# Joined compress products, a norm shift in halves, and a reordered router in a two-block transformer kernel

## The chip, the core and the metric

The kernel runs on one core of one Trainium2 chip. The core has five engines with instruction streams of their own: TensorE (PE, matrix products and transposes; its weight loads are listed apart as PEld), VectorE (DVE), ScalarE (ACT), GpSimd (POOL) and SyncE (SP), which issues most DMAs. They wait for each other by semaphores. The metric is the device time of one execution in microseconds (us); lower is better.

## The reference

256 tokens of width 1024 pass through two layers of a first block and one layer of a second, all in fp32:

```python
for l in range(2):
    mix = retention(h, ...) if l == 0 else nsa_attention(h, ..., shared)
    h = layer_norm(ALPHA * h + mix, ln_mix_g[l], ln_mix_b[l])
    h = layer_norm(ALPHA * h + moe(h, ...), ln_ffn_g[l], ln_ffn_b[l])
# moe: 16 experts, each token's two are chosen inside the best of four groups
aff = sigmoid(x @ router_w);  sel_score = aff + router_b
y  += w[:, e:e+1] * ((silu(x @ w_gate[e]) * (x @ w_up[e])) @ w_down[e])
# nsa, ahead of layer 1's attention: 15 overlapping pieces of 32 tokens a group are compressed
blk = t[:, cidx] + pe;  k_cmp, v_cmp = gelu(blk @ w1) @ w2      # once for keys, once for values
```

The second block has an input projection of 8192 columns, two kinds of attention, a gated output, and a feed-forward part with a short convolution.

## The kernel before, in words

The 256 tokens are two tiles of 128 (`tt` 0 and 1). A weight matrix is read in blocks of 512 rows and 512 columns. Each block is split in two: ACT rounds it to a high part `whi` (L497), DVE subtracts that for a low part `wlo` (L503). The activations are split likewise into `th` and `tl`, so that a product of fp32 precision is the sum of three (whi x th, wlo x th, whi x tl), four of each for a block and a tile. `steady_tensor` runs such a stage; its first column group has line L698, the others L714. PE takes high parts from five places and raw or low parts from seven, in the order of the program.

Ahead of each stage the tokens are normalised and turned. `centre_half` takes mean and variance, ACT the square root (`root_half`, L817, after loading its table, L813), DVE the reciprocal (L821) and the shift (`shift_half`, L838), one instruction of 1024 columns for a tile. `half_turn_tensor` (L766) then transposes eight pieces of 128 columns; ACT copies them to `th` (L773, or L789 where a gain is applied), DVE subtracts to get `tl` (L781, L799). `opened_by` says at which steps of the next stage's first column group PE waits for them.

Behind the experts the order is: the last expert product (L1466), `centre_half` from the accumulators (L2825 to L2830), root, shift, turn of tile 0, the first column group's products for tile 0, turn of tile 1, the products for tile 1. The weights of the first two blocks are split by ACT there too, ahead of the table load.

At a router (`router_tensor_logits`, `router_vector`) PE forms 16 logits for a token from th and tl (L1127, L1132), turns tile 1 between the tiles, and then puts row sums of X into the accumulators (L1137). DVE takes the score (L1164), picks the experts in a chain of short operations up to `picked_r` (L1207), normalises their weights (L1212 to L1215), and builds selection matrices from slot numbers (L1218, L1236). PE gathers the tokens with them (L1403) out of `xn_h` and `xn_l`, the high and low part of X, whose low part DVE subtracts in two pieces (L2806). The experts' weights come through 20 places (`moe_homes`), each with a condition of its own; SP issues them in order.

The compress part (`nsa_in_tensor`, `nsa_beside_tensor`, L2113 and the lines around it) multiplies `cmp_x`, 60 columns of pieces, by four blocks of first-layer weights, in plain fp32, two for keys into one accumulator bank and two for values into another. The trace counts such a product as two instructions. Each half then has its own gelu on ACT (L2163), transposes (L2079) and second-layer product (L2091 for keys, L2098 for values). Between them stand transposes of queries (L2045), gate products (L2130) and the first attention scores (L2301). The order on every engine is written out by hand, by the counters `n` of the functions that stand beside a stage.

## Time and profile before

| what | before |
|---|---|
| median of 3 runs | 1333.68 us (1333.26 to 1333.89) |
| profiled execution: own time | 1332.24 us |
| profiled execution: span | 1330.1 us |
| PE busy | 1278.3 us (96%), 6630 instructions |
| PE weight loads | 890.9 us (67%) |
| DVE busy | 736.7 us (55%) |
| ACT busy | 541.0 us (41%) |
| DMA | 342.51 MB, 258 GB/s mean |

The span is the time between the first and the last instruction of the profiled execution; its own time has what lies around it. PE's busy time is modelled at the ends of products, so that a share of 96% still holds short waits. In the trace a row's first number is a start in us from the span's start, the second a duration; `x8` means eight instructions together, and the bracket the idle time of the engine ahead of the row and what ended it.

### The profile page before, as it was taken

How to read it: one execution, taken by the hardware profiler on the slowest of the kernel's cores; microseconds unless marked ns; L12 is line 12 of the kernel's file. 1: busy time of each engine (PE TensorE's matmuls, PEld its weight loads, DVE VectorE, ACT ScalarE, POOL GpSimd, SP SyncE). 2: the span in 40 equal slices, each digit the busy share in tenths (PEclk: the TensorE clock that was granted, in tenths of full speed). 3: DMA queues.
4: the chain of work that ended last, by engine and by line, in shares of the span. 5: the costliest groups of instructions: out<-in, count | busy, mean ns of one | idle time of the engine just before them, and what ended most of it. 6: DMA issues, size and time to landing. Idle time of an engine off the chain costs nothing.

```text
span 1330.1 us, 16620 instructions
## 1 busy us (share of the span) xinstructions
PE 1278.3 (96%) x6630; PEld 890.9 (67%) x6630; DVE 736.7 (55%) x1231; ACT 541.0 (41%) x791; POOL 74.9 (6%) x78
## 2 busy tenths in 40 slices
PE   9999998999999799998999999699999999999998
PEld 8887886444443477676444443378888887899986
DVE  4866657233222685876333322565674557688772
ACT  4455443111111443682111112455556655555551
POOL 0000000000000000000000000005770000000000
PEclk9999998999999899898999999899999999999999
DMA  9653588999999665407999999765455434655540
GB/s 335 234 177 127 159 343 328 407 420 421 421 422 417 217 202 188 183 17 301 393 421 421 421 421 421 283 190 165 148 159 160 157 127 149 215 167 183 190 158 32
DMA packets 103890, 342.51 MB, mean 258 GB/s; under 512 B 10188, under 2 KB 17020, under 8 KB 79100
## 3 DMA queue, kind: packets, MB, share of 16 engines
q1 hardware_dynamic: 100992, 336.30, 67.2%
q10 hardware_dynamic: 2812, 5.04, 1.1%
q8 instruction: 57, 0.93, 0.3%
q14 instruction: 29, 0.24, 0.0%
HBM read 340.27 MB, written 1.05 MB: 257 GB/s over the span
## 4 chain that ended last, share of the span: by engine, by line
PE 83%; DVE 10%; ACT 4%; issue 2%; ACTq 1%; DMA 0%; DVEq 0%; SPq 0%
PE PS L714 24%; PE PS L1421 17%; PE PS L1455 9%; PE PS L566 6%; PE PS L635 6%; PE PS L613 5%; PE PS L1403 2%; DVE wlo L503 2%; PE PS L1466 2%; ACT whi L497 1%; PE PS L698 1%; PE PS L2113 1%; PE PS L531 1%; PE PS L766 1%; PE PS L1866 1%
## 5 line engine op out<-in xcount | busy, mean ns | idle before, releaser
L503 DVE TENSOR_TENSOR wlo<-raw,whi 128x2048 fp32r<-128x2048 f32 (+1 forms) x122 | 272.9, 2254 | 106.2 <-ACT whi L497 101.8
L497 ACT ACTIVATE whi<-raw 128x2048 fp32r<-128x2048 f32 (+1 forms) x122 | 225.0, 1875 | 22.3 <-PE PS L613 13.9
L714 PE MATMUL PS<-whi,th 128*128 128x512 f32 x480 | 191.1, 398 | 1.2 <-ACT a_proj L3042 0.9
L714 PE MATMUL PS<-whi,tl 128*128 128x512 f32 x480 | 187.3, 390 | 0.0
L714 PE MATMUL PS<-wlo,th 128*128 128x512 f32 x480 | 186.9, 389 | 0.0
L1421 PE MATMUL PS<-moe_ring,xg 128*64 128x512 f32 x640 | 142.0, 593 | 2.6 <-DVE slot_sum L1579 2.6
L1421 PEld LDWEIGHTS PS<-moe_ring,xg 128*64 128x64 f32 x640 | 46.5, 137 | 91.6 <-issue 91.6
L1593 DVE TENSOR_TENSOR hidden<-hidden,PS 64x256 f32<-64x256 f32 x32 | 13.5, 423 | 170.0 <-ACT hidden L1536 170.0
L714 PEld LDWEIGHTS PS<-whi,th 128*128 128x128 f32 x480 | 90.2, 188 | 21.7 <-issue 2.0
L714 PEld LDWEIGHTS PS<-whi,tl 128*128 128x128 f32 x480 | 90.1, 188 | 19.2
L714 PEld LDWEIGHTS PS<-wlo,th 128*128 128x128 f32 x480 | 90.2, 188 | 17.5
L1563 DVE SCALAR_TENSOR_TENSOR y_split<-PS,w_slot,y_split 64x512 fp32r<-64x512 f32 x60 | 45.0, 749 | 93.7 <-ACT y_split L1519 92.8
L1536 ACT ACTIVATE hidden<-PS 64x512 f32<-64x512 f32 x32 | 18.9, 590 | 183.2 <-PE PS L1421 183.2
L566 PE MATMUL PS<-th,whi 128*128 128x256 f32 x288 | 81.7, 284 | 1.5 <-DVE wlo L503 1.5
L566 PE MATMUL PS<-th,wlo 128*128 128x256 f32 x288 | 81.5, 283 | 0.0
L566 PE MATMUL PS<-tl,whi 128*128 128x256 f32 x288 | 81.5, 283 | 0.0
L1519 ACT ACTIVATE y_split<-PS,w_slot 64x512 fp32r<-64x512 f32 x60 | 40.9, 682 | 97.1 <-PE PS L1455 96.4
L1455 PE MATMUL PS<-moe_ring,hT 128*64 128x512 f32 x320 | 72.6, 598 | 0.0
L903 POOL TENSOR_TENSOR rope_t<-b_proj,trig 128x256 f32<-128x256 f32 x48 | 41.5, 896 | 307.0 <-issue 294.0
L566 PEld LDWEIGHTS PS<-th,whi 128*128 128x128 f32 x288 | 55.3, 192 | 1.9 <-DVE wlo L503 1.4
L566 PEld LDWEIGHTS PS<-th,wlo 128*128 128x128 f32 x288 | 55.3, 192 | 0.0
L566 PEld LDWEIGHTS PS<-tl,whi 128*128 128x128 f32 x288 | 55.3, 192 | 0.0
(436 smaller groups left out, 2144.4 us busy)
## 6 DMA issues: line engine op xcount, KB each, us to landing
moe_ring<-in_moe_w_gate SPq DMA_DIRECT2D x40, 1024.0 KB, 13.8
moe_ring<-in_moe_w_up SPq DMA_DIRECT2D x40, 1024.0 KB, 15.9
moe_ring<-in_moe_w_down SPq DMA_DIRECT2D x40, 1024.0 KB, 19.3
raw<-in_w_in SPq DMA_DIRECT2D x32, 1024.0 KB, 5.3
raw<-in_ret_w_in SPq DMA_DIRECT2D x24, 1024.0 KB, 5.9
raw<-in_w_up SPq DMA_DIRECT2D x20, 1024.0 KB, 5.2
raw<-in_w_down SPq DMA_DIRECT2D x10, 1024.0 KB, 5.0
raw<-in_ret_w_out SPq DMA_DIRECT2D x8, 1024.0 KB, 5.1
```

The lines of the kernel that those rows point to most:

```text
L497: nc.scalar.activation(s.whi[:, high, 0:kc, 0:wide], s.raw[:, slot, 0:kc, 0:wide], ACT.Copy).then_inc(s.hi_done, 1)
L503: nc.vector.tensor_tensor(s.wlo[:, slot, 0:kc, 0:wide], s.raw[:, slot, 0:kc, 0:wide], s.whi[:, high, 0:kc, 0:wide], ALU.subtract).then_inc ...
L566: last = nc.tensor.matmul(PS[:, up_bank(j) + m // 2, (m % 2) * SEQ:(m % 2 + 1) * SEQ], w[:, k, c, m * P:(m + 1) * P], x[:, KC * kb + c, :] ...
L613: last = nc.tensor.matmul(PS[:, bank(j, tt), :], x[:, at, tt * P:(tt + 1) * P], w[:, k, c, :], start=(kb == 0 and c == 0 and i == 0), stop ...
L635: last = nc.tensor.matmul(PS[:, bank(j, tt), :], x[:, at, tt * P:(tt + 1) * P], w[:, k, c, :], start=(not opened and kb == 0 and c == 0 an ...
L714: last = nc.tensor.matmul(PS[:, 2 * (col % 2) + tt, 0:wide], x[:, KC * kb + c, tt * P:(tt + 1) * P], w[:, k, c, 0:wide], start=(kb == 0 an ...
L903: o(nc.gpsimd.tensor_tensor(t[i], u, v, ALU.mult))
L1403: last = nc.tensor.matmul(PS[:, bank, (c % 2) * SEQ:(c % 2 + 1) * SEQ], x[:, tt, c * P:(c + 1) * P], pick[:, g % 2, tt, :, :], start=(i == ...
L1421: m = nc.tensor.matmul(PS[64 * k:64 * k + 64, gate_up_bank(e), :], x, moe_place(layer, n)[:, c, :], start=(half == 0 and c == 0), stop=(ha ...
L1455: m = nc.tensor.matmul(PS[64 * half:64 * half + 64, down_bank_of(e), :], hT_of(e)[:, 2 * b + c, :], moe_place(layer, down_at(e) + b)[:, 2 ...
L1519: nc.scalar.activation(y_of(e)[rows, half, :], PS[rows, down_bank_of(e), :], ACT.Identity, scale=w_slot[rows, e:e + 1]).then_inc(s.y_hi, 1)
L1563: nc.vector.scalar_tensor_tensor(y_of(e)[low, half, :], PS[rows, down_bank_of(e), :], w_slot[rows, e:e + 1], y_of(e)[rows, half, :], ALU.m ...
```

## The change

Five things are edited.

1. The key and value products of the compress part go by turns into one bank, keys into rows 0 to 63 (60 and a pad of zeros), values into rows 64 to 123. One gelu, one pair of transposes and one group of copies serve both; both second-layer products stand behind the first half of the gate products. The four weight blocks are loaded as key, value, key, value.
2. The shift is two instructions of 512 columns with a semaphore each; the turn of the first half waits for the first. Behind the experts ACT loads the table ahead of the weight split, and takes the root between the two splits. In the first column group PE does the eight high-weight products of tile 0's second block, then the turn of tile 1, then the four low-weight products.
3. Behind each expert layer, 14 products of zeros stand ahead of the first turn.
4. At a router the row sums of tile 0 stand ahead of tile 1's turn; the low parts of X stand behind the picks, one ahead of each selection; the weights are normalised behind both selections. The `gains` place of the experts is used ahead of `rows`.
5. ACT issues the compress parameters behind the first weight split of the key stage, and two groups of parameters of the second block inside its input stage.

```diff
                      ("raw", 3), ("high", 1), ("raw", 4), ("high", 2), ("raw", 5), ("high", 3), ("raw", 6), ("high", 4),
-                     ("rows", 0), ("gains", 0), ("turned", 0), ("turned", 1)]
+                     ("gains", 0), ("rows", 0), ("turned", 0), ("turned", 1)]
...
+                    pe.wait_ge(half_lo, 4 * k + 1)
+                if step == 1:
                     pe.wait_ge(half_lo, 4 * k + 2)
-                if step == 1 and turn is not None:
+                if step == "turn":
                     turn()
...
+                        if tt == 0 and kb == 1 and high_first:
+                            pe.wait_ge(hi_done, b + 1)
+                            for c in range(KC):
+                                for x in (xh, xl):
+                                    nc.tensor.matmul(out, x[:, KC + c, 0:P], whi[:, b % HIGHS, c, :], start=False, stop=False)
+                            opening("turn")
+                            pe.wait_ge(lo_done, b + 1)
+                            for c in range(KC):
+                                last = nc.tensor.matmul(out, xh[:, KC + c, 0:P], wlo[:, b % RAWS, c, :], start=False,
+                                                        stop=(c == KC - 1))
+                            continue
...
+                    if half == 1 and late is not None:
+                        late(tt)
...
+        def normed_turn_tensor(pe, turn, k, tt):
+
+            half_turn_tensor(pe, turn, tokens(X), lambda tt: pe.wait_ge(half_normed, k + tt + 1), (tt,),
+                             lambda tt: pe.wait_ge(normed, k + tt + 1))
...
         def shift_half(tt):
-            nc.vector.scalar_tensor_tensor(X[:, tt, :], X[:, tt, :], small[:, 8 + tt:9 + tt], gb[:, 1, :],
-                                           ALU.mult, ALU.add).then_inc(normed, 1)
-
-        def layer_norm_halves(dve, st, o, k):
-
-            dve.wait_ge(params_in, 16 * st.params)
-            for tt in range(TT):
-                centre_half(o, tt)
-                inverse_half(dve, o, k, tt)
-                shift_half(tt)
+            for h, done in ((0, half_normed), (1, normed)):
+                x = X[:, tt, 512 * h:512 * h + 512]
+                nc.vector.scalar_tensor_tensor(x, x, small[:, 8 + tt:9 + tt], gb[:, 1, 512 * h:512 * h + 512],
+                                               ALU.mult, ALU.add).then_inc(done, 1)
...
+        def row_sums_tensor(tt):
+
+            for half in range(2):
+                last = nc.tensor.matmul(PS[:, 2 * tt + half, :], ident_a[:, :], X[:, tt, half * BW:(half + 1) * BW],
+                                        start=True, stop=False, skip_group_check=True)
+            return last
+
+        def busy(n):
+            zeros = nc.const_aps.tensor(0.0, [P, P], F32)
+            for _ in range(n):
+                nc.tensor.matmul(PS[:, 7, 0:P], zeros, zeros, start=True, stop=True)
...
                 if tt == 1:
-                    half_turn_tensor(pe, k, tokens(X), normed_by(pe, 4 * layer), (1,))
+                    pe.wait_ge(acc_free, 2 * (l_ret_out, l_nsa_out)[layer].n0 + 3)
+                    row_sums_tensor(0)
+                    normed_turn_tensor(pe, k, 4 * layer, 1)
...
-            for tt in range(TT):
-                for half in range(2):
-                    last = nc.tensor.matmul(PS[:, 2 * tt + half, :], ident_a[:, :], X[:, tt, half * BW:(half + 1) * BW],
-                                            start=True, stop=False, skip_group_check=True)
-            last.then_inc(rows_summed, 1)
+            row_sums_tensor(1).then_inc(rows_summed, 1)
...
+            def token_low(h):
+                dve.wait_ge(xn_h_done, 3 * layer + h + 2)
+                nc.vector.tensor_tensor(straight(xn_l, 1)[:, h], neighbours(X, 1)[:, h], straight(xn_h, 1)[:, h],
+                                        ALU.subtract).then_inc(xn_l_done, 1)
...
+            token_low(0)
+            inbox(dve, st)
+
+            o.then(nc.vector.scalar_tensor_tensor(rt2.rearrange("p t e -> p (t e)"), PS[:, 6, 0:TT * E], 1.0,
+                                                  picked_r[:, :, :].rearrange("p t e -> p (t e)"), ALU.add, ALU.mult))
+            selection(paired, 0, layer, rt2, 1)
+            token_low(1)
+            inbox(dve, st)
+            o(nc.vector.tensor_reduce(top[0][:, 0:1], PS[:, 7, 0:E], AX.X, ALU.max))
+            xg_copy(dve, paired, layer, 0, 1, first_bank(1))
+            selection(paired, 1, layer, rt2, 1)
             o.then(nc.vector.tensor_tensor(w_tok, affinity, picked_r[:, :, :], ALU.mult))
             o.then(nc.vector.tensor_reduce(top[2], w_tok, AX.X, ALU.add))
             o.then(nc.vector.reciprocal(top[3], top[2]))
-            o(nc.vector.tensor_tensor(w_tok, w_tok, wide(top[3], P, TT, E), ALU.mult))
-            inbox(dve, st)
-
-            o.then(nc.vector.scalar_tensor_tensor(rt2.rearrange("p t e -> p (t e)"), PS[:, 6, 0:TT * E], 1.0,
-                                                  picked_r[:, :, :].rearrange("p t e -> p (t e)"), ALU.add, ALU.mult))
-            selection(paired, 0, layer, rt2, 1)
-            inbox(dve, st)
-            o(nc.vector.tensor_reduce(top[0][:, 0:1], PS[:, 7, 0:E], AX.X, ALU.max))
-            selection(paired, 1, layer, rt2, 1)
             o(nc.vector.tensor_scalar(slot_no, rt2, -1.0, None, ALU.add))
+            o.then(nc.vector.tensor_tensor(w_tok, w_tok, wide(top[3], P, TT, E), ALU.mult))
             o.then(nc.vector.tensor_copy(w_split[:, :, :, 0], w_tok))
             o(nc.vector.tensor_tensor(w_split[:, :, :, 1], w_tok, w_split[:, :, :, 0], ALU.subtract))
             o(nc.vector.tensor_copy(slot_r[:, :, :], slot_no))
...
-                src = a["cmp_k_w1" if i < 2 else "cmp_v_w1"][D * (i % 2):D * (i % 2) + D, :]
+                src = a[("cmp_k_w1", "cmp_v_w1")[i % 2]][D * (i // 2):D * (i // 2) + D, :]
...
+                pe.wait_ge(tables_copied, COPIED_GELU)
+                for c in range(2):
+                    last = nc.tensor.transpose(PS[:, 7, 256 + c * P:256 + c * P + 124],
+                                               cmp_g[0:124, c * P:(c + 1) * P], cst[0:124, C_ID:C_ID + 124])
+                last.then_inc(tables_turned, 1)
...
-            for i in range(4):
-                k = i // 2
-                pe.wait_ge(lo_done, cmp_b0 + i + 1)
-                if i % 2 == 0:
-                    pe.wait_ge(cmp_built, BUILT_KW if k else BUILT_KS)
+            pe.wait_ge(cmp_built, BUILT_KW)
+            for h in range(2):
+                pe.wait_ge(lo_done, cmp_b0 + 2 * h + 2)
                 for c in range(8):
-                    last = nc.tensor.matmul(PS[0:60, 4 if k else 7, 0:CMP_HID], cmp_x[:, k, 8 * (i % 2) + c, 0:60],
-                                            cmp_block(i)[:, c, :], start=(i % 2 == 0 and c == 0),
-                                            stop=(i % 2 == 1 and c == 7))
-                last.then_inc(block_used, 1)
-                nsa_beside_tensor(pe, 10 + i)
+                    for k in range(2):
+                        last = nc.tensor.matmul(PS[64 * k:64 * k + 64 - 4 * k, 7, 0:CMP_HID],
+                                                cmp_x[:, k, 8 * h + c, 0:64 - 4 * k], cmp_block(2 * h + k)[:, c, :],
+                                                start=(h == 0 and c == 0), stop=(h == 1 and c == 7),
+                                                skip_group_check=True)
+                        if c == 7:
+                            last.then_inc(block_used, 1)
+            nsa_beside_tensor(pe, 12)
...
+            def keys_beside(n):
+                if n == 0:
+                    for dst, src in cmp_params():
+                        act.dma_start(dst, src).then_inc(tables_in, 16)
+                nsa_beside_scalar(act, n)
+            steady_side(act, l_nsa_kv, nsa_split_hi, nsa_kv_evacuate, keys_beside)
...
-            for b in range(AHEAD):
-                split_hi(act, sweep_first, moe_b0[layer] + b, 0)
             early_table(ACT.Sqrt)
+            split_hi(act, sweep_first, moe_b0[layer], 0)
+            root_half(act, 2 + 4 * layer, 0)
+            split_hi(act, sweep_first, moe_b0[layer] + 1, 0)
...
-            half_turn_tensor(pe, 2, tokens(X), normed_by(pe, 2), (0,))
-            nsa_in_tensor(pe, opened_by(pe, 2, lambda: half_turn_tensor(pe, 2, tokens(X), normed_by(pe, 2), (1,))))
+            busy(14)
+            normed_turn_tensor(pe, 2, 2, 0)
+            nsa_in_tensor(pe, opened_by(pe, 2, lambda: normed_turn_tensor(pe, 2, 2, 1)))
...
+            def a_in_beside(n):
+                if n == 1:
+                    params(act, st, a_params())
+                if n == 3:
+                    for dst, src in conv_params():
+                        act.dma_start(dst, src).then_inc(tables_in, 16)
+            steady_side(act, l_a_in, split_hi, take(l_a_in, lambda j, tt: a_proj[:, j, tt, :] if j < 2 else a_v[:, tt, :]),
+                        a_in_beside)```

On ACT, behind the experts of layer 0. `small` holds a token's statistics, `raw` the weight block as it came. Before:

```order
L497 ACTIVATE whi<-raw 128x2048 x2
L813 ACT_TABLE_LOAD
L813 ACTIVATE small<-cst 128x1
L817 ACTIVATE small<-small 128x1
L773 ACTIVATE th<-PS 128x4x128 x2
L817 ACTIVATE small<-small 128x1
L2734 DMA n_c<-in_c_nsa 128x292
L773 ACTIVATE th<-PS 128x4x128 x2
L3016 DMA cmp_pe<-in_cmp_pe_k 16x2x64 x2
L3016 DMA cmp_pe<-in_cmp_pe_v 16x2x64 x2
L3016 DMA cmp_w2k<-in_cmp_k_w 128x2x64 x2
L3016 DMA cmp_w2v<-in_cmp_v_w 128x2x64
```

After, from the same place on:

```order
L832 ACT_TABLE_LOAD
L832 ACTIVATE small<-cst 128x1
L499 ACTIVATE whi<-raw 128x2048
L836 ACTIVATE small<-small 128x1
L499 ACTIVATE whi<-raw 128x2048
L791 ACTIVATE th<-PS 128x4x128 x2
L836 ACTIVATE small<-small 128x1
L2771 DMA n_c<-in_c_nsa 128x292
L791 ACTIVATE th<-PS 128x4x128 x2
L499 ACTIVATE whi<-raw 128x2048
L2203 DMA cmp_pe<-in_cmp_pe_k 16x2x64 x2
L2203 DMA cmp_pe<-in_cmp_pe_v 16x2x64 x2
```

The table load went ahead of both splits, the root between them, and the compress DMAs behind the next split.

On PE, from the last query transposes' neighbours at the compress part to the first gate products. `cmp_g` is the gelu's output, `cst` holds the identity. Before:

```order
L2045 MATMUL PS<-cst,n_q 128x128 x8
L2113 MATMUL PS<-raw,cmp_x 60x256 x24
L2079 MATMUL PS<-cst,cmp_g 128x60 x2
L2045 MATMUL PS<-cst,n_q 128x128 x8
L2113 MATMUL PS<-raw,cmp_x 60x256 x8
L2091 MATMUL PS<-cmp_h,cmp_w2k 128x60 x2
L2130 MATMUL PS<-th,whi 48x256
```

After, from the last of 32 products by turns on:

```order
L2144 MATMUL PS<-raw,cmp_x 64x256
L2144 MATMUL PS<-raw,cmp_x 60x256
L2079 MATMUL PS<-cst,n_q 128x128 x8
L2117 MATMUL PS<-cst,cmp_g 128x124 x2
L2163 MATMUL PS<-th,whi 48x256
```

The products stand together; one pair of transposes serves keys and values; the second-layer product of the keys, L2091 before, is behind the first twelve gate products.

On DVE at a router, from the picks to the second selection matrix. Before:

```order
L1207 SCALAR_TENSOR_TENSOR picked_r<-route,tops 128x16 x2
L1212 TENSOR_TENSOR route<-route,picked_r 128x32
L1213 TENSOR_REDUCE tops<-route 128x2
L1214 RECIPROCAL tops<-tops 128x2
L1215 TENSOR_TENSOR route<-route,tops 128x32
L1218 SCALAR_TENSOR_TENSOR route<-PS,picked_r 128x32
L1236 TENSOR_TENSOR pick<-cst,route 128x256 x2
L1222 TENSOR_REDUCE tops<-PS 128x1
L1236 TENSOR_TENSOR pick<-cst,route 128x256 x2
```

After:

```order
L1236 SCALAR_TENSOR_TENSOR picked_r<-route,tops 128x16 x2
L1184 TENSOR_TENSOR xn_l<-X,xn_h 128x512
L1244 SCALAR_TENSOR_TENSOR route<-PS,picked_r 128x32
L1268 TENSOR_TENSOR pick<-cst,route 128x256 x2
L1184 TENSOR_TENSOR xn_l<-X,xn_h 128x512
L1249 TENSOR_REDUCE tops<-PS 128x1
L1589 COPY xg<-PS 128x512
L1268 TENSOR_TENSOR pick<-cst,route 128x256 x2
L1252 TENSOR_TENSOR route<-route,picked_r 128x32
```

One low part of X stands ahead of each selection, and the normalising of weights behind both.

## Rows read from the trace of the kernel before

**Rows 1.** PE's waits: what waited for what, us in total, times, longest.

```profile
PE PS L766 <- DVE X L838: 16.0, 4, 5.1
...
PE PS L698 <- DVE tl L799: 2.6, 1, 2.6
```

**Rows 2.** Timeline behind the experts of layer 0: start us, us, engine, line, operation.

```profile
440.97 3.71 ACT L497 ACTIVATE whi<-raw 128x2048 fp32r<-128x2048 f32 x2
...
444.33 1.27 DVE L2830 SCALAR_TENSOR_TENSOR X<-PS,small,gb 128x1024 f32<-128x1024 f32 x1
...
446.52 1.28 DVE L838 SCALAR_TENSOR_TENSOR X<-X,small,gb 128x1024 f32<-128x1024 f32 x1
...
448.17 1.97 PE L766 MATMUL PS<-cst,X 128*128 128x128 f32 x8 [5.05 <-DVE X L838]
...
450.80 0.69 DVE L781 TENSOR_TENSOR tl<-PS,th 128x512 fp32r<-128x512 f32 x1 [0.16 <-ACT th L773]
...
455.63 2.28 DVE L503 TENSOR_TENSOR wlo<-raw,whi 128x2048 fp32r<-128x2048 f32 x1
...
462.24 3.72 ACT L497 ACTIVATE whi<-raw 128x2048 fp32r<-128x2048 f32 x2 [4.34 <-issue]
```

**Rows 3.** The chain of waits in order of time: start us, us, what.

```profile
227.88 4.10 PE PS L1403 x32
...
255.65 6.87 PE PS L1421 x32
...
451.60 4.74 PE PS L698 x12
...
466.69 5.73 PE PS L714 x24
...
530.15 1.41 PE PS L2130 x12
...
874.04 27.48 PE PS L714 x120
```

**Rows 4.** Timeline of DVE behind the experts of layer 1.

```profile
856.10 2.16 DVE L799 SCALAR_TENSOR_TENSOR tl<-PS,small,th 128x128 fp32r<-128x128 f32 x8 [0.50 <-ACT th L789]
...
861.19 1.28 DVE L838 SCALAR_TENSOR_TENSOR X<-X,small,gb 128x1024 f32<-128x1024 f32 x1
```

**Rows 5.** Timeline of PE and DVE at the compress part.

```profile
514.12 10.57 PE L2113 MATMUL PS<-raw,cmp_x 128*60 128x256 f32 x48
...
518.60 0.42 DVE L892 TENSOR_TENSOR n_q<-rope_t 128x256 f32<-128x256 f32 x1
...
524.88 1.09 PE L2045 MATMUL PS<-cst,n_q 128*128 128x128 f32 x8
...
529.50 0.66 PE L2091 MATMUL PS<-cmp_h,cmp_w2k 128*128 128x60 f32 x4
...
533.19 1.29 DVE L2455 TENSOR_REDUCE n_top<-PS 128x2 f32<-128x512 f32 x2 [0.47 <-PE PS L2310]
...
534.61 1.10 PE L2098 MATMUL PS<-cmp_w2v,cmp_hr 128*60 128x64 f32 x16
...
536.16 1.13 PE L2301 MATMUL PS<-n_kp,n_qT 64*128 64x512 f32 x4 [0.45 <-ACT n_gT L2006]
```

**Rows 6.** Timeline: a weight load of an expert, value products of attention.

```profile
255.48 0.14 PEld L1421 LDWEIGHTS PS<-moe_ring,xg 128*64 128x64 f32 x2 [0.28 <-issue]
...
551.13 1.09 PE L2349 MATMUL PS<-n_pT,n_vp 128*64 128x128 f32 x16
```

**Rows 7.** Timeline of DVE and PE at the router of layer 0.

```profile
218.61 2.08 DVE L2806 TENSOR_TENSOR xn_l<-X,xn_h 128x512 fp32r<-128x512 f32 x2 [0.32 <-ACT xn_h L2785]
...
220.43 5.07 PE L1137 MATMUL PS<-X,small 128*128 128x512 f32 x8
...
220.62 0.23 DVE L1164 TENSOR_REDUCE route<-PS 128x32 f32<-128x64 f32 x1
```

**Rows 8.** One window: PE, PEld, DVE, ACT, POOL busy, PE's granted clock, DMA.

```profile
222.00:224.00 2.00, 2.00 (x4) 0.78 (x3) 1.77 (x11) 0.00 (x0) 0.00 (x0) 0.69 0.70 287
```

117 lines of the change are left out of this document (48 added, 69 removed).

## The prediction

> **What bounds the kernel now.** I read the page first: TensorE (PE) is busy for 96% of the span, so a change can win only where PE stands still or where it does less. The view of PE's waits says where it stands still, and no DMA is named there. Four turns of a normalised tile wait for the shift L838 (16.0 us in all), and the first products behind the experts of layer 1 wait 2.6 us for a low half [rows 1]. In the rows behind layer 0 [rows 2] the reader is to see one chain: ScalarE (ACT) splits two weight blocks (440.97, 3.71), only then loads the table for the square root, VectorE (DVE) has had the centred tile since 445.60 (444.33 + 1.27) and starts the shift at 446.52; the turn follows at 448.17. DVE then does a low split (2.28 each), two low halves of the turned tile (the second ends at 451.49), and 4.14 later, at 455.63, the next low split. The chain of waits [rows 3] shows PE's side: 12 products from 451.60 in 4.74, and the next column group at 466.69. The same shape stands behind layer 1 [rows 4]. Last I read the compress products [rows 5] beside other products of half width [rows 6], and the router [rows 7, 8].
>
> **The change part by part.** All times below are of the profiled execution (own time 1332.24, span 1330.1); the median of the runs is 1333.68, 1.44 above it.
>
> *Behind the experts, layer 0.* The table load and the root go ahead of the second weight split, so the root is ready before DVE has centred the tile. The shift then starts 0.20 behind 445.60 (a reciprocal between), at 445.8, and not at 446.52. It comes in two halves of about 0.65 (half of 1.28 [rows 2]), so the turn of the first half starts near 446.8, and copying to the high half is done before DVE has its low split behind it: 447.1 + 2.28 = 449.4. The low halves take 0.69 each: 449.4 to 450.8. PE's opening now waits for the first one alone, so it starts at 450.1 instead of 451.60. The second low split follows as before 4.14 behind the low halves, at 454.9, and ends at 457.2. Before, PE did 36 products behind that split: 12 of tile 0, 24 of tile 1. Now the eight products of high weights of tile 0 and the turn of tile 1 stand ahead of the wait for the split; the two low halves of tile 1 go on to 458.6, and 24 products at 0.229 (27.48 for 120 [rows 3]) end at 464.2. The next group stood at 466.69. Gain 2.4. It is set by DVE, so that it hardly depends on the clock: with the opening products at the 0.395 that the 12 of [rows 3] show (the granted clock was down for part of them), the loss is about 1.0. What is late next is the low split of the block after the next. Seven DMA issues on ACT, for which it did nothing else for 4.34 ahead of the split at 462.24 [rows 2], are moved between the two splits of that row (1.86 each). The first split now stands at 457.9, behind the copies of tile 1's turn; the issues, some 4.9 with the one that lay beside the copies, run to 464.7, the second split to 466.6 and its low half to 468.9. PE wants that at 464.2 + 24 x 0.229 = 469.7. I price it at nothing; if the cover of 0.8 is gone, it costs as much as the issues run over.
>
> *Fourteen zero products ahead of the first turn.* The trace counts an fp32 product as two instructions, so 28. Bounds: half of the 0.22 of a 256-column instruction (10.57 for 48 [rows 5]) is 0.11, 3.1 in all; a transposing instruction of that width takes 0.136 (1.09 for eight), 3.8. PE is free from 443.1 (448.17 less the wait of 5.05 [rows 2]), so they end between 446.2 and 446.9, and the turn is ready at 446.5 to 446.8. I take nothing; the far end costs 0.4, and at half clock 3.
>
> *Behind the experts, layer 1.* The same steps. The shift moves 0.7 up; the eight low halves (856.10 to 858.26 [rows 4]) follow the low split, whose place moves as far, and now run 855.0 to 857.2. PE starts after four of them, near 856.2. The second shift, 2.93 behind the low halves in the old rows (861.19 less 858.26), stands at 860.1, its low split ends at 863.65, the low halves of tile 1 at 865.85, and 24 products at 0.229 end at 871.4. The next group stood at 874.04 [rows 3]. It also needs its own high and low parts; the DMA issues that stood ahead of them on ACT are moved behind, so those end near 870.5. Gain 2.5; 0.6 less if all products run at half clock.
>
> *Joined compress products.* Before: 64 instructions with 60 output columns, 0.22 each, 48 of them together [rows 5], the other 16 after two groups of transposes. Now keys go to rows 0 to 63 of one bank and values to rows 64 to 123, by turns. No row of before shows this shape. The nearest on one side is the experts' first product, which goes to two halves of a bank by turns: 6.87 for 32 instructions of 512 columns, 0.215 each [rows 3], half of the 0.44 that twice the 0.22 would be, and its weight loads come in twos [rows 6]. On the other side the value products of attention, of 128 columns and by turns to two halves too: 16 in 1.09, 0.07 each against 0.11 [rows 6]. Between 128 and 512 columns lies 256: 0.108 each, 3.5 for a half of 32. The other bound is the old 0.22. I take 0.108, since both neighbours run at that pace. From 514.12: first half to 517.6. The second half waits for marks that DVE gives only behind the rope of the second query group, which ends at 519.0 (518.60 + 0.42 [rows 5]); so it runs 519.2 to 522.7. Then the query transposes 1.09, the gelu's two (0.3), twelve gate products 1.41, both second-layer products 0.66 and 1.10, and the first scores 1.13 [rows 3, 5]: 528.4, and with hand-overs the maximum L2455 at 529.0. It stood at 533.19 [rows 5]. Gain 4.2. The second-layer product of the values (1.10) is only moved up, ahead of the first scores, and it is in the sum on both sides: I put nothing more for its absence later, where PE stands between softmax steps.
>
> *Routers, both layers.* Three edits help the score L1164, at 220.62 [rows 7]: the shift in halves (0.65), the low halves of X (2.08 from 218.61, to 220.69) out of DVE's way, and row sums on PE ahead of tile 1. They bring 1.2 to 1.9 in each layer. Two things go back. One low half (1.04) now stands behind the picks; what left that place (four short operations that normalise weights, each below the 0.23 of L1164, together some 0.7) doesn't cover it, so 0.3 is lost. And the eight row sums (5.07 from 220.43) ran until the picks were nearly done; the granted clock was 0.69 in 222 to 224, on its way back [rows 8], and the gather that follows took 4.10 for 32 [rows 3], 0.128 each. Now four of them are gone from there, PE stands idle for some 3 us before the gather, and I expect part of the gather at half clock, which loses about 1.3, a third of its 4.10. Sum per router 0.1, both 0.2; bounds -1 and +2 each. The expert blocks' transfers aren't among PE's waits, and the order of two of their places is changed so that one starts earlier: nothing.
>
> Sum: 2.4 + 2.5 + 4.2 + 0.2 = 9.3. 1332.24 - 9.3 = 1322.9; against the median 1333.68 - 9.3 = **1324.4**.
>
> The Trainium skill ("TensorE: Matmul & The Clock Gate", Part 3: Packing small matmuls, The mechanism) says that a weight load overlaps products in flight only where the row groups differ. Both halves of the joined product use the same 128 rows. By that rule loads and products would stand one after another. The rows of the experts' product, also on the same rows, speak against it: 0.215 a piece, with the loads inside it; the trace does not agree with the rule here.
>
> **The rivals.**
>
> *A: the clock comes back for the gather.* The row sums ahead of tile 1 fill PE's wait for the shift; if the clock doesn't fall there, the logits take less and the gather keeps its 4.10. For it: PE's rows before the fall are dense. Against it: three short idle stretches remain. It gives 1.3 back in each layer and some 0.5 of the logits: 3.7 more, 1320.7.
>
> *B: the joined products run one after another.* For it: no row has 64 and 60 columns by turns at 256. Against it: the experts' pairs [rows 3]. 64 x 0.22 = 14.1 from 514.12 end at 528.3 rather than 522.7: 5.6 less, 1330.0.
>
> *C: slower than before, by loads that are not hidden.* Place: the 64 joined instructions. Each then costs its load (0.14 for two of the experts' [rows 6], taken here for one) and its columns (0.22): 64 x 0.36 = 23.0, ending at 537.1, 14.4 less: 1338.8. The kernel is slower than before once the products end 9.3 later than forecast, at 532.0: a pace above (532.0 - 514.12) / 64 = 0.28. Against it: with loads of as many columns the experts' pairs take 0.215 for twice the moving columns.
>
> **How the numbers follow.** The forecast as reckoned 0.62, with a range of its own of 1321 to 1328 (the half-clock prices of both layers' ends, 1.6, on one side, and the routers' bounds); A 0.12, B 0.12, C 0.04; 0.10 for several terms short at once, 1328 to 1334. A measurement of this kernel tells changes above 0.2% (2.7 us) from none: faster is under 1331.0. Faster: 0.62 + 0.12 + 0.09 of B + 0.04 of the rest = 0.87. Same: 0.03 of B and 0.05 of the rest, 0.08. Slower: C and 0.01, 0.05. Range 1319.5 to 1330: A below and the near half of B above are in it, C is not.
>
> **What would show it.** In the profile of the changed kernel: the four waits for the shift (16.0 in all) shrink to under 5, those behind the experts to near zero, as PE has zero products there; the next column groups stand 2.4 and, from the same stage's start, 2.5 nearer to the last expert product; 64 compress instructions span about 8.6 with a gap of 1.6 in the middle; the gather takes over 5 where A is wrong and 4.1 where it is right. The prediction is wrong if the compress products take over 12, if PE waits for a weight block behind the moved DMA issues, or if the zero products end after the shift's first half.

## The result, and the profile of the changed kernel

| | before | changed |
|---|---|---|
| median of 20 runs, us | 1333.62 (1331.81 to 1335.18) | 1335.85 (1334.61 to 1340.75) |
| profiled execution: own time, span | 1332.24, 1330.1 | 1336.96, 1335.2 |
| ratio, 95% interval | | 1.0018 [1.0012, 1.0025] |

The change made the kernel 0.18% slower. The forecast was 1324.4, so 11.5 us are missing (14.1 between the profiled executions, 1336.96 against 1322.9).

In the kernel before, the last expert products of the two layers stood here, so that the turns came 5.06 behind their ends, 443.11 and 848.71:

```profile
441.94 1.17 PE L1466 MATMUL PS<-y_last,pickT 128*128 128x512 f32 x4 [1.31 <-DVE y_last L1563]
...
847.54 1.17 PE L1466 MATMUL PS<-y_last,pickT 128*128 128x512 f32 x4 [1.31 <-DVE y_last L1563]
```

Behind the experts of layer 0 the timeline of the changed kernel (start us, us, engine, line, operation) reads as follows; it answers to [rows 2]:

```profile
443.33 1.16 PE L1499 MATMUL PS<-y_last,pickT 128*128 128x512 f32 x4 [1.31 <-DVE y_last L1598]
...
448.17 1.28 DVE L2863 SCALAR_TENSOR_TENSOR X<-PS,small,gb 128x1024 f32<-128x1024 f32 x1 [2.37 <-issue]
...
449.67 5.42 PE L1140 MATMUL PS<-const-float32-0.0 128*128 128x128 f32 x28 [5.18 <-issue]
...
454.93 1.04 PE L784 MATMUL PS<-cst,X 128*128 128x128 f32 x8
...
470.86 0.39 PE L730 MATMUL PS<-whi,th 128*128 128x512 f32 x1
```

PE's last expert product ends at 444.49. Then it waits 5.18, and the wait bears no engine's name but "issue": time in which the engine waited for nothing that the profile shows. Only then do the zero products run, for 5.42, and the first turn stands 10.44 behind the experts, where it stood 5.06 behind them. DVE has a wait of the same kind, 2.37. The last row is the first product of the next column group, at 466.69 before [rows 3]. Layer 1 answers to [rows 4]:

```profile
845.64 1.16 PE L1499 MATMUL PS<-y_last,pickT 128*128 128x512 f32 x4 [1.32 <-DVE y_last L1598]
...
851.93 2.71 PE L1140 MATMUL PS<-const-float32-0.0 128*128 128x128 f32 x11 [5.13 <-issue]
...
856.25 4.00 PE L1140 MATMUL PS<-const-float32-0.0 128*128 128x128 f32 x17 [1.60 <-issue]
...
860.04 1.09 PE L784 MATMUL PS<-cst,X 128*128 128x128 f32 x8
...
880.57 0.39 PE L730 MATMUL PS<-whi,th 128*128 128x512 f32 x1
```

Here the wait comes twice, once ahead of the zero products and once in their midst, and the turn stands 13.24 behind the experts. PE's waits answer to [rows 1]; of the 16.0 us for the shift 1.2 are left, as forecast, and 11.9 without a named engine stand in their place:

```profile
PE PS L1140 <- issue: 11.9, 3, 5.2
...
PE PS L784 <- DVE X L859: 1.2, 2, 0.6
```

The chain of waits (start, us, what) answers to [rows 3]: the gathers of the two layers, and the 24 products that end the first column group in either layer (of a new line, L714; the next column group is L730):

```profile
227.09 6.26 PE PS L1436 x32
...
465.29 5.73 PE PS L714 x24
...
629.13 6.60 PE PS L1436 x32
...
873.38 7.35 PE PS L714 x24
```

The compress part answers to [rows 5]. From the first joined product to the maximum L2492 it takes 532.94 - 518.22 = 14.72, against 533.19 - 514.12 = 19.07:

```profile
518.22 3.67 PE L2144 MATMUL PS<-raw,cmp_x 128*64 128x256 f32 x32
...
523.79 3.67 PE L2144 MATMUL PS<-raw,cmp_x 128*64 128x256 f32 x32 [1.90 <-DVEq L2065]
...
532.94 1.29 DVE L2492 TENSOR_REDUCE n_top<-PS 128x2 f32<-128x512 f32 x2 [1.57 <-PE PS L2346]
```

Taken by stages between the two profiled executions (plus is lost): up to the last expert product of layer 0 +1.4, from there to the next column group +2.8, compress and attention -6.4 (4.35 of it the compress part), router and experts of layer 1 +0.3, the end of layer 1's experts +8.4, the rest -1.4. The sum, +5.1, is the difference of the spans.

### The profile page after: what moved, and what is told of

Its sections match the earlier page's. It is cut to its first block, busy times and chain, and to the rows that moved or that the text cites. A ratio compares the mean times of both kernels' runs of the same rounds, so it can differ in the third digit from the quotient of the medians.

```text
span 1335.2 us, 16742 instructions
## 1 busy us (share of the span) xinstructions
PE 1280.2 (96%) x6684; PEld 895.0 (67%) x6684; DVE 738.0 (55%) x1240; ACT 540.9 (41%) x790; POOL 74.9 (6%) x78
## 4 chain that ended last, share of the span: by engine, by line
PE 84%; DVE 10%; ACT 3%; issue 2%; DMA 0%; DVEq 0%; ACTq 0%; SPq 0%
PE PS L730 23%; PE PS L1454 17%; PE PS L1488 9%; PE PS L568 6%; PE PS L637 6%; PE PS L615 5%; PE PS L1436 2%; PE PS L714 2%; PE PS L1499 2%; DVE wlo L505 2%; PE PS L533 1%; PE PS L1140 1%; PE PS L1900 1%; PE PS L1874 1%; DVE ff_u L2731 1%
## 5 line engine op out<-in xcount | busy, mean ns | idle before, releaser
L499 ACT ACTIVATE whi<-raw 128x2048 fp32r<-128x2048 f32 (+1 forms) x122 | 225.4, 1876 | 17.9 <-PE PS L615 13.9
L730 PE MATMUL PS<-whi,th 128*128 128x512 f32 x480 | 190.9, 398 | 0.2 <-DVE wlo L505 0.2
L730 PE MATMUL PS<-whi,tl 128*128 128x512 f32 x480 | 187.3, 390 | 0.0
L730 PE MATMUL PS<-wlo,th 128*128 128x512 f32 x480 | 186.9, 389 | 0.0
L730 PEld LDWEIGHTS PS<-whi,th 128*128 128x128 f32 x480 | 90.2, 188 | 19.9 <-issue 1.3
L730 PEld LDWEIGHTS PS<-whi,tl 128*128 128x128 f32 x480 | 90.1, 188 | 19.1
L730 PEld LDWEIGHTS PS<-wlo,th 128*128 128x128 f32 x480 | 90.2, 188 | 17.7
L1598 DVE SCALAR_TENSOR_TENSOR y_split<-PS,w_slot,y_split 64x512 fp32r<-64x512 f32 x60 | 45.0, 749 | 93.8 <-ACT y_split L1554 92.8
```

The lines of the kernel that those rows point to most:

```text
L499: nc.scalar.activation(s.whi[:, high, 0:kc, 0:wide], s.raw[:, slot, 0:kc, 0:wide], ACT.Copy).then_inc(s.hi_done, 1)
L730: last = nc.tensor.matmul(PS[:, 2 * (col % 2) + tt, 0:wide], x[:, KC * kb + c, tt * P:(tt + 1) * P], w[:, k, c, 0:wide], start=(kb == 0 an ...
L1598: nc.vector.scalar_tensor_tensor(y_of(e)[low, half, :], PS[rows, down_bank_of(e), :], w_slot[rows, e:e + 1], y_of(e)[rows, half, :], ALU.m ...
```

## The experiments

My theory: the wait called "issue" is the code. Between the experts and the first turn stands a long part for overfull experts, which these inputs skip by a taken jump; the instructions behind the jump have to come from memory first. In the kernel before, the same arrival lay beside the shift, so that it cost little; the zero products can't start until it has come and push the turn back by their own length. The rivals: the clock (the half clock behind the experts makes the loss), and DVE's chain (the turn waits for the shift anyway).

The traces show the arrival itself. The page lists instruction queues beside the DMA queues (packets, MB, share of 16 engines' time). Between 447 and 449 the changed kernel has one packet of queue q8, and between 445 and 447 the kernel before has one:

```profile
q8 instruction: 1, 0.02, 3.5%
...
q8 instruction: 1, 0.02, 3.5%
```

A share of 3.5% of 16 engines in 2 us is 1.1 us. In narrower windows the packets start at 447.1 and 445.6, both 2.5 to 2.6 behind the last expert product. So they land at about 448.2 and 446.7, and PE's next instruction, the zero product in one kernel and the turn in the other, starts 1.4 later in both. In layer 1 of the changed kernel there are two such packets, from 849.4 and 853.9, and the products that had waited start 1.4 behind the landing of each. Without the jump (e2, 443 to 451) and with the part set aside (e9, 444 to 451) queue q8 has no packet there.

The columns for layers 0 and 1 are from the end of the last expert product to the next column group's start, worked out from rows like those above. They come from the one traced execution of each kernel, which can lie off its median: 1321.43 us for e2, 1327.45 for e5, 1329.19 for e9, 1327.85 for e11. The kernel before was timed again beside each group of runs, and the ratios go by those times (medians 1333.71 for e1 to e4, 1334.08 for e5 to e8, 1334.52 for e9 to e12).

| run | median us | ratio to before, 95% interval | layer 0 | layer 1 |
|---|---|---|---|---|
| before | 1333.62 | | 23.58 | 25.33 |
| changed | 1335.85 | 1.0018 [1.0012, 1.0025] | 26.37 | 33.77 |
| e1 no zero products | 1329.50 | 0.9964 [0.9952, 0.9976] | 23.73 | 26.30 |
| e2 no jump | 1326.54 | 0.9950 [0.9936, 0.9963] | 20.80 | 22.58 |
| e3 no zero products, row sums as before | 1328.19 | 0.9958 [0.9945, 0.9972] | 23.78 | 26.29 |
| e4 before without the jump | 1333.81 | 1.0000 [0.9991, 1.0009] | 23.92 | 25.03 |
| e5 hint | 1331.51 | 0.9975 [0.9964, 0.9986] | 25.79 | 26.79 |
| e6 before with joined compress part | 1331.34 | 0.9965 [0.9952, 0.9979] | 25.17 | 26.07 |
| e7 hint, zero products in the routers | 1329.08 | 0.9961 [0.9949, 0.9974] | 26.63 | 23.08 |
| e8 zero products ahead of the jump | 1331.30 | 0.9979 [0.9969, 0.9988] | 24.95 | 29.51 |
| e9 part set aside | 1324.32 | 0.9925 [0.9911, 0.9939] | 21.21 | 25.82 |
| e10 as e9, no zero products | 1325.94 | 0.9940 [0.9927, 0.9954] | 22.40 | 25.56 |
| e11 as e9, row sums as before | 1321.18 | 0.9902 [0.9888, 0.9915] | 22.63 | 25.85 |
| e12 before with zero products | 1345.19 | 1.0084 [1.0070, 1.0098] | 29.36 | 34.79 |

**e1: the changed kernel without the zero products.**

```
-            busy(14)
             normed_turn_tensor(pe, 2, 2, 0)
...
-            busy(14)
             normed_turn_tensor(pe, 4, 6, 0)
```

> The changed kernel without the 14 zero products behind each expert layer. Code theory: behind the experts every engine jumps past the part for overfull experts, PE's code behind the jump arrives 5.1 to 5.2 us after its last expert product, and the zero products only start then. Without them the first turn starts 5.1 to 5.2 behind the last expert product in both layers (now 10.4 and 13.2), the next column group comes about 3.2 (layer 0) and 6 to 9 (layer 1) nearer, total 1324 to 1327. Clock theory (the losses behind the experts are products at half clock): without the zero products the clock is lower still, the first column group takes longer, total 1335 to 1338.

1329.50, 6.35 less than the changed kernel: the zero products, priced at nothing, cost more than half of what was missing. The clock rival had expected the time to stay. But 1329.50 is above the 1324 to 1327 of the theory. The wait stays. In layer 0 DVE has one of its own, so that the shift comes late and the turn stands 5.88 behind the experts; in layer 1 the wait is the turn's, 5.15:

```profile
447.70 1.28 DVE L2863 SCALAR_TENSOR_TENSOR X<-PS,small,gb 128x1024 f32<-128x1024 f32 x1 [2.38 <-issue]
...
449.89 1.97 PE L784 MATMUL PS<-cst,X 128*128 128x128 f32 x8 [5.88 <-DVE X L859]
...
845.73 1.17 PE L1499 MATMUL PS<-y_last,pickT 128*128 128x512 f32 x4 [1.31 <-DVE y_last L1598]
...
852.04 1.97 PE L784 MATMUL PS<-cst,X 128*128 128x128 f32 x8 [5.15 <-issue]
```

**e2: the changed kernel without the part for overfull experts and its jumps, on all engines** (the part never runs on these inputs).

```
             crowded = paired_tensor(pe, paired, layer)
-            with pe.If(crowded > 0):
-                joined(pe, sweep_second[layer], 1)
...
```

> The changed kernel with the zero products but without the part for overfull experts and without its branch on all engines (that part never runs on these inputs). Code theory: no wait for code, the zero products start within 0.3 us of the last expert product and end 3 to 4 later, the first turn starts 3.3 to 4.0 behind the last expert product; the prediction's gains of 2.4 and 2.5 against the kernel before come true; total 1317 to 1321. Clock theory: the branch is free, the 5.2 us stay, total 1335 to 1337.

The wait is gone in both layers: the zero products follow the experts at once, take 3.28 at a granted clock of 1.00, and lie beside the shift, which now sets the turn. The steps of the prediction come out in the traced execution: 23.58 - 20.80 = 2.8 in layer 0 and 25.33 - 22.58 = 2.75 in layer 1, where it had 2.4 and 2.5.

```profile
442.39 1.17 PE L1499 MATMUL PS<-y_last,pickT 128*128 128x512 f32 x4 [1.31 <-DVE y_last L1598]
...
443.40 3.28 PE L1140 MATMUL PS<-const-float32-0.0 128*128 128x128 f32 x28
...
446.96 1.32 PE L784 MATMUL PS<-cst,X 128*128 128x128 f32 x8 [0.28 <-DVE X L859]
...
464.36 0.39 PE L730 MATMUL PS<-whi,th 128*128 128x512 f32 x1
...
841.26 1.17 PE L1499 MATMUL PS<-y_last,pickT 128*128 128x512 f32 x4 [1.31 <-DVE y_last L1598]
...
865.01 0.39 PE L730 MATMUL PS<-whi,th 128*128 128x512 f32 x1
```

The median, 1326.54, is 5.5 us above the upper end of what I expected; the traced execution is the fastest of five, 1321.43. The routers, below, are part of the gap, and the rest is open.

**e3: without the zero products, and with all row sums behind the logits again.**

```
-                    row_sums_tensor(0)
                     normed_turn_tensor(pe, k, 4 * layer, 1)
...
+            row_sums_tensor(0)
             row_sums_tensor(1).then_inc(rows_summed, 1)
```

> The changed kernel without the zero products and with all eight row-sum instructions behind the logits again, as before. Clock at the router: with PE busy until the picks, the gather starts at full clock and takes 4.1 in both layers (now 6.26 and 6.60); against the run without zero products alone 3.5 to 4.5 less, total 1320 to 1323. Rival (the gather is slow because the low halves of X come late behind the picks, or because of its weight loads): it stays above 6, no gain against that run, or a loss of up to 0.5.

1328.19, ratio 0.9958 [0.9945, 0.9972]. Both gathers are back at 4.09, but this and e1 can't be told apart by their intervals. In layer 0 the first expert product starts 1.3 earlier than in e1, in layer 1 no earlier: the 1320 to 1323 that I expected are missed by 5, and what the early row sums cost isn't shown here.

**e4: the kernel before without the part and its jumps** (edit as in e2).

> The kernel before without the part for overfull experts and without its branch. Code theory: in it too the first turn behind the experts waits for code, hidden all but 0.3 behind the shift: PE starts the turn 5.06 behind its last expert product in both layers, 0.37 after the shift ends, and 0.06 after it at the routers. Without the jump the turn starts 0.05 to 0.1 after the shift, and the total falls by 0.5 to 1. Shift theory (the wait was for the shift alone): 0.37 stays, total the same.

1333.81, ratio 1.0000 [0.9991, 1.0009]. In the kernel before the jump cost nothing that the time shows; the 0.5 to 1 that I expected didn't come. The turn starts 0.06 behind the shift's end (447.52 + 1.28), where it started 0.37 behind in [rows 2] (446.52 + 1.28 = 447.80, turn at 448.17). So in the kernel before the code was the later of the two waits, by about 0.3, although the row names the shift.

```profile
447.52 1.28 DVE L838 SCALAR_TENSOR_TENSOR X<-X,small,gb 128x1024 f32<-128x1024 f32 x1
...
448.86 1.97 PE L766 MATMUL PS<-cst,X 128*128 128x128 f32 x8 [4.76 <-DVE X L838]
```

**e12: the kernel before with the zero products alone.**

```
+            busy(14)
             half_turn_tensor(pe, 2, tokens(X), normed_by(pe, 2), (0,))
...
+            busy(14)
             half_turn_tensor(pe, 4, tokens(X), normed_by(pe, 6), (0,))
```

> The kernel before with the 14 products of zeros alone, ahead of the first turn behind the experts of both layers. By the prediction's step they lie in time in which TensorE waits anyway: no change, 1333 to 1334, or up to 2 less by the clock. If they can start only when the code behind the jump is there, the turn starts 5.1 + 3.3 = 8.4 us behind the last expert product in place of 5.05: 3.3 us lost at each layer, less what the clock gives back: 1336 to 1340.

1345.19, 10.7 slower than the kernel before, and above what I had expected: at layer 1 the code comes in two pieces, with waits of 5.10 and 3.18, and the zero products run at a granted clock of 0.50. The turn stands 14.58 behind the experts there. This is the failed step by itself, in the kernel before.

```profile
851.82 1.17 PE L1466 MATMUL PS<-y_last,pickT 128*128 128x512 f32 x4 [1.31 <-DVE y_last L1563]
...
858.09 2.50 PE L2858 MATMUL PS<-const-float32-0.0 128*128 128x128 f32 x10 [5.10 <-issue]
...
863.78 4.00 PE L2858 MATMUL PS<-const-float32-0.0 128*128 128x128 f32 x18 [3.18 <-issue]
...
867.57 1.91 PE L766 MATMUL PS<-cst,X 128*128 128x128 f32 x8
```

**e8: the zero products ahead of the jump.**

```
             crowded = paired_tensor(pe, paired, layer)
+            busy(14)
             with pe.If(crowded > 0):
...
-            busy(14)
```

> The changed kernel with the 14 products of zeros ahead of the jump in place of behind it. If the sequencer takes the jump only when the products ahead of it have gone, the code comes 5.1 us behind the last product of zeros and the turn 8.4 behind the last expert product: 1335 to 1337, as the changed kernel. If it runs ahead and the fetch lies beside the products of zeros, the turn comes 5.2 behind the last expert product at a full clock: 1326 to 1329.

Between the two: 1331.30. The zero products run at once and the wait follows them, 4.10 from their end (445.89) to the turn, in layer 1 4.08. So 3.29 of products queued ahead of the jump hide about 5.2 - 4.1 = 1.1 us of the arrival, no more. The packet agrees: it starts at 447.4, 1.5 behind the last product, not 2.6. That the sequencer runs no further ahead of the products than this is my reading; no run measures its lead by itself.

```profile
442.60 3.29 PE L1140 MATMUL PS<-const-float32-0.0 128*128 128x128 f32 x28
...
449.98 1.09 PE L784 MATMUL PS<-cst,X 128*128 128x128 f32 x8 [4.10 <-issue]
```

**e5: the changed kernel with a hint, ahead of the last two experts, that the jump will be taken.**

```
+                if e == E - 2:

...
-            with pe.If(crowded > 0):
+            eng.br_eq(flag, 0, f"on_{name}", f"more_{name}").branch_hint(hint)
```

> The changed kernel whole, with one instruction more on TensorE and on VectorE, 24 to 48 products ahead of the jump past the part for overfull experts: a hint to its sequencer that the jump will be taken. If the wait behind the last expert product is the arrival of the code behind the jump, it goes: the zero products start within 0.3 us of the last product's end in both layers, the next group of keys and values starts about 21 us behind that end as in the run without the jump (26.5 and 32 in the changed kernel), and the time is 1326 to 1328 us. If the wait is anything else (the clock, the statistics, the shift), nothing moves and it stays at 1335 to 1337.

The hint shows the nature of the wait but doesn't mend it, and 1331.51 is above the 1326 to 1328 that I expected. On PE in layer 0 the wait is gone; in layer 1 the first piece is there at once and the second isn't, 4.04 in the midst of the zero products. On DVE the hint made it worse in layer 0, 4.97 where 2.37 had been, and now DVE holds the turn up. Why the hint hurt there I did not test. The runs fall into two groups, four at 1327, the traced one among them, and eight at 1331 to 1334.

```profile
442.74 3.29 PE L1140 MATMUL PS<-const-float32-0.0 128*128 128x128 f32 x28
...
446.58 1.30 DVE L2875 BATCH_NORM_STATS2 small<-PS 128x6 f32<-128x512 f32 x2 [4.97 <-issue]
...
849.47 3.18 PE L1140 MATMUL PS<-const-float32-0.0 128*128 128x128 f32 x18 [4.04 <-issue]
```

**e7: the hints, and zero products in the routers** (2 behind the second turn, 6 behind the late row sums).

```
                     normed_turn_tensor(pe, k, 4 * layer, 1)
+                    busy(2, 5)
...
             row_sums_tensor(1).then_inc(rows_summed, 1)
+            busy(6)
```

> The run with the hints, and in each router 2 products of zeros behind the second turn and 6 behind the late row sums, in time in which TensorE waits. If what the early row sums cost is the clock alone, the gathers of the first experts go from 5.7 to 6.6 us back to 4.1 with the scores as early as they are: 3 to 4 us less than the run with the hints, 1322 to 1324. If the products of zeros are late for the counts behind them (they take 0.47 us each at half clock), each layer loses up to 0.7: 1327 to 1329.

1329.08, ratio 0.9961 [0.9949, 0.9974], above the 1322 to 1324 of the first expectation: the row sums now ran at full clock (1.96 for four, 3.26 in e5), and the score came 0.2 earlier than in e5, but PE then stood idle for 2.6 us until the picks, and the gather ran at a granted clock of 0.50 again. The time is 2.4 below e5 in the medians, with intervals that overlap; no more can be read from it. The pieces of code fall elsewhere in this longer program: layer 0 now has a wait of 2.61 within its zero products, layer 1 none.

```profile
226.20 6.73 PE PS L1438 x32
```

**e6: the kernel before with the joined compressed keys and values alone** (the change's edits from L2014 to L2319, with the buffer cmp_g).

> The kernel before with the joined compressed keys and values alone. By the prediction's step it gains 4.2 us, by the trace of the changed kernel 4.35: 1329.2 to 1329.6. If the joining also takes away the stretch at half clock in the attention behind it, 2 us more: about 1327.3. If the gain in the changed kernel came from a state of the clock that the zero products brought, less than 4: 1330 or more.

1331.34, ratio 0.9965 [0.9952, 0.9979]; six runs, two at 1327.0 and four at 1330.9 to 1332.6, so that the gain is 2.7 in the medians, 2.8 to 6.4 by the interval, and short of the expected 4.2. In the trace the joined products take 3.67 twice, as in the changed kernel, and the part from them to the maximum 530.63 - 516.27 = 14.36, 4.7 less than before. What is missing was lost elsewhere in this execution: behind the experts it takes 25.17 and 26.07, 1.6 and 0.7 more than before, though nothing is edited there; why isn't shown. So the joined part gains what was forecast without the zero products, but the kernel's time doesn't show all of it. The granted clock in the attention behind it is 0.50 here, 0.67 and 0.50 in the kernel before, 1.00 in the changed one: in these executions the 2 us that the changed kernel gains there are not the joining's.

```profile
516.27 3.67 PE L2111 MATMUL PS<-raw,cmp_x 128*64 128x256 f32 x32
...
521.47 3.67 PE L2111 MATMUL PS<-raw,cmp_x 128*64 128x256 f32 x32 [1.53 <-DVEq L2032]
...
530.63 1.29 DVE L2454 TENSOR_REDUCE n_top<-PS 128x2 f32<-128x512 f32 x2 [1.57 <-PE PS L2308]
```

**e9: the whole changed kernel, with the part for overfull experts written at the end of PE's and DVE's programs.** The test stands where it stood; these inputs fall through it.

```
-            with pe.If(crowded > 0):
+            eng.br_cond(flag > 0, f"more_{name}", f"on_{name}")
+            on = nc.switch_body(f"on_{name}", parent=ahead, valid_engines=[eng.engine])
...
+            put_aside(pe, "PE")
```

> The changed kernel whole, with the part for overfull experts written at the end of TensorE's and of VectorE's program, so that these inputs fall through the test and no jump is taken behind the experts. If the wait is the code behind the taken jump, it goes on both engines and at both layers: products of zeros 0.3 us behind the last expert product, the first turn 4.5 behind it, keys and values 21 behind it, 1325 to 1328 us, as the run without the part. If the test itself (a register, a compare) makes the wait, 5 us stay and so does the time, 1335 to 1337.

1324.32: the forecast of the change, 1324.4, met by the whole computation. That it is met to 0.1 is partly luck: in the traced execution the router of layer 0 lost 1.0 and the end of layer 1's experts 0.5, where 0.1 and 2.5 of gain were forecast. No PE wait called "issue" is left ahead of the zero products in either layer, and none on DVE. The test itself costs nothing that shows.

```profile
443.80 3.28 PE L1140 MATMUL PS<-const-float32-0.0 128*128 128x128 f32 x28
...
447.37 1.32 PE L784 MATMUL PS<-cst,X 128*128 128x128 f32 x8 [0.29 <-DVE X L859]
```

**e10: as e9, without the zero products** (edit as in e1).

> The run with the part set aside, without the 14 products of zeros. By the prediction's step they cost nothing where the code is there, and give back part of a half clock behind them: the same time as the run with the part set aside or up to 3 us more, 1326 to 1330. If they hold the turn up here too, 1 to 3 us less: 1323 to 1325.

1325.94, 1.6 more than e9, with intervals that overlap. With the code there the turn waits 3.40 for the shift and runs at half clock, 1.97 instead of 1.32. So here the zero products do lie in time that PE waits anyway. In the traces they gain 1.2 in layer 0 and lose 0.3 in layer 1; a gain in time isn't shown. What made them cost in the changed kernel was that PE had no code to run them.

```profile
446.77 1.97 PE L784 MATMUL PS<-cst,X 128*128 128x128 f32 x8 [3.40 <-DVE X L859]
```

**e11: as e9, with all row sums behind the logits** (edit as in e3).

> The run with the part set aside, with all row sums behind the logits again as in the kernel before. The gathers of the first experts take 4.1 us again (5.7 to 6.6 with half the row sums early), the logits come some 1.4 to 2.4 later. If the early row sums lose more than they give, 1 to 2 us less than with the part set aside: 1324 to 1326. If the two are even, the same.

1321.18, the fastest, 0.98% below the kernel before. The gathers take 4.09 at a granted clock of 1.00, where e9 has 6.69 at 0.50 in the same two microseconds, though its score comes 2.0 earlier. The first expert product of layer 0 starts at 232.12 against 232.77. Five of six runs lie at 1320.2 to 1322.0; the profiled one, 1327.85, has a granted clock of 0.50 in most of 1098 to 1106 and of 534 to 542. The gathers of e9 and of this run:

```profile
226.15 6.69 PE PS L1436 x32
...
228.10 4.09 PE PS L1435 x32
```

## Why the prediction was wrong

*The zero products, "I take nothing": this step failed.* It rested on "PE is free from 443.1 (448.17 less the wait of 5.05 [rows 2])". PE was idle from there, not free: its next instruction started 5.1 to 5.2 us behind the last expert product (layer 1 of e1, e12, the changed kernel), because its code had not come. The row ascribes the 5.05 to the shift, but the shift had ended 0.37 ahead of the turn, and the packet of code landed 1.4 ahead of it, as in the changed kernel: two waits ran side by side, and the row names the one that ended first. The zero products so started 5.2 and 5.1 us later than I had put them and took 5.42 and 2.71 + 4.00, partly at half clock, where I had 3.1 to 3.8. They ended at 455.09, about 5 us behind the shift's first half, which was one of the prediction's own signs of being wrong.

Against the steps' forecast the ends of the two layers lost 2.4 + 2.8 = 5.2 and 2.5 + 8.4 = 10.9. Of these 16.1 the zero products make 2.6 and 7.5 (the changed kernel less e1); the other 6.0 is the wait itself, on PE and in layer 0 on DVE too, behind which an earlier shift gains nothing, and what the clock took there. The prediction gave slower than before 0.05 in all, and its rival C named a mechanism that isn't there.

The Trainium skill ("Runtime: NRT & Kernel Launch", section Instruction fetch mechanics) says that a taken branch to a page that isn't at hand stops the engine until the page has been fetched. The trace agrees, and gives the price: 5.1 to 5.2 on PE, 2.4 on DVE, and a second wait of 1.6 to 4.0 on PE where a second packet followed. Over the whole span of the changed kernel the queue of PE's waits has:

```profile
q8 instruction: 57, 0.93, 0.3%
```

57 packets of 0.93 MB are 16 KB each.

*Behind the experts, 2.4 and 2.5: right, and hidden.* With the wait taken out by e2 they measure 2.8 and 2.75; in e9, 2.4 in layer 0 and -0.5 in layer 1, where the last 24 products ran partly at half clock (7.36 against 5.73 in e2) and most of 12 others at a granted clock of 0.50. The forecast had 0.6 for that; between e2 and e9 it is 3.2.

*Compress, 4.2: right.* 4.35 in the changed kernel, 4.7 in e6, at a pace of 3.67 / 32 = 0.115 where I took 0.108. Rivals B and C are out. Its second half starts behind DVE's mark with a gap of 1.90, forecast 1.6.

*Routers, 0.2 gained: mis-sized.* The score came 1.4 and 2.4 earlier, counted from the statistics of the second tile, but the gathers took 6.26 and 6.60 where 4.10 stood [rows 3] and where I had allowed 5.4. From there to the last expert product layer 0 lost 1.0 and layer 1 0.3. Rival A is out. Between e9 and e11 the early row sums lose 3.1 in the medians, between e1 and e3 1.3, each time with intervals that overlap: the slow gather is shown, its price in time only roughly.

*The DMA issues moved on ACT, priced at nothing:* right. In e9, as in the changed kernel, the second split follows 2.08 in which ACT did its issues, and PE's products of the next column group start without a wait for a block.

## What to carry to other kernels

A row names one wait, and another may lie under it; before putting work into an idle stretch, ask whether the engine could have issued it at all, and look for a gap between the end of what is named and the start of the waiting instruction, here 0.37 where 0.06 is usual, and for packets of the instruction queue. Code that hardly ever runs belongs at the program's end, so that the usual path falls through: that alone turned the same change from 0.2% slower to 0.75% faster. The hint on the jump tried here was no substitute: it left a wait of 4.04 on PE in layer 1 and brought one of 4.97 on DVE in layer 0.

## What the runs showed of the hardware that I had not expected

- 3.3 us of products queued ahead of the jump hid only 1.1 us of the code's arrival (e8), a third of their length.
- A jump can cost a second wait: behind the experts of layer 1 the same 28 instructions had one of 1.60 (changed, behind 11 of them), 3.18 (e12, behind 10), 4.04 (e5, behind 18) or none (e7). In the changed kernel and in e12 a second packet of the queue starts 4.5 and 5.8 us behind the first; what sets that distance isn't shown.
- Times of one kernel lie up to 7 us apart (e11: 1320.2 and 1327.9). The mean granted clock of e11's slowest run is 0.980, that of the others 0.986 to 0.988, and its trace has a granted clock of 0.50 in most of 534 to 542 and 1098 to 1106. Whether the others lack these stretches isn't shown, as one execution of each kernel was traced. Differences of 2 to 3 us between versions need more runs than the five or six made here.
